# The 31-tap depthwise convolution of a three-block network: which engines compute its four channel pairs

## The chip, the cores and the metric

One core of one Trainium2 chip runs the whole program. The metric is the time of one execution on the device in microseconds (us), the median of several. A core has five engines with queues of their own: TensorE (PE: matrix multiplication, with weight loads shown as PEld), VectorE (DVE), ScalarE (ACT), GpSimd (POOL) and SyncE (SP, which here only issues DMAs). They run side by side and order each other by semaphores.

## The reference, cut to what matters

The network is three blocks on 256 positions and 1024 channels, all float32. The change lies in the first block's second layer, a Conformer convolution module:

```python
def conformer_conv(h, pw1_w, pw1_b, dw_w, dw_b, ln_g, ln_b, pw2_w, pw2_b):
    u = h @ pw1_w + pw1_b
    a, gt = jnp.split(u, 2, axis=-1)
    c = causal_dwconv(a * jax.nn.sigmoid(gt), dw_w, dw_b)
    c = jax.nn.silu(layernorm(c, ln_g, ln_b))
    return c @ pw2_w + pw2_b
```

`causal_dwconv` has 31 taps for each channel: output position t is the sum over s of 0 to 30 of the input at t-s times the tap weight of that channel for s. The layer norm goes over the channels, so it needs the convolution of all 1024 channels before it can start.

## The kernel before, in words

Activations lie feature-major in SBUF: a tile is 128 channels by 256 positions, and the 1024 channels are eight tiles, in four pairs q = 0 to 3 (tiles 2q and 2q+1). Nearly all buffers are 256-wide slices of one SBUF tensor, the arena. Weights of 1 MB units stream from HBM through a ring of eight slots (`weight_ring`). SP issues a unit as soon as PE has used up the unit whose slot it takes. The third block ends in a mixture of 64 experts whose weights stream through the same ring and through the arena in transfers of 2 MB.

The order on each engine is written out by hand. In the Conformer stage it is this.

PE (`conf_pe`, L1431): the gated projection pw1 in eight column pairs (the first two in a sweep while the norm before it ends, L1432, then pairs 2 to 7, L1433 to L1435). Even pairs are the gate, odd pairs the value; value pair 2q+1 completes channel pair q. Then a projection of the memory that a later attention needs (`xa_k1` pair 2, L1436). Then the convolution of channel tiles 6 and 7 as matrix products (L1439 to L1442): for each tap and tile a diagonal matrix of the tap's weights, times the shifted input, summed in PSUM bank 4. Then two more memory projections (`xa_k1` 3, `xa_v1` 0), the products with a matrix of ones that sum all eight convolved tiles for the mean (L1446 to L1452), `xa_v1` 1, the sums of squares (L1454, `norm_pe` L398), and pw2.

ACT: for each q a sigmoid of the gate (L1477), and for q = 0 to 2 the base of the convolution, `conf_base_act` (L1457): input times the weight of the tap s=0, plus the bias, into the tile pair `CV`. The 62 diagonal matrices (two tiles by 31 taps) are built by ACT much earlier, in the feed-forward stage (L1344, `diag`). After the products ACT takes the two tiles out of PSUM (L1485).

DVE (`conf_dve`, L1534): for each q the gated product (`glu_dve`, L1509) and behind it a portion of the convolution of pairs 0 to 2 (`conv_taps_dve`, L1514). Each of the 30 further taps is two scalar_tensor_tensor instructions, one for each tile of the pair: tile += shifted input times tap weight, both inputs in SBUF (L1526). Before each tap DVE waits for its own tap before (`own.wait()`). In total 180 such instructions. Then come the mean (L1542), its subtraction (L1546) and the layer norm.

POOL (`conf_pool`, L1157): only the short sums of squares of the norms (`sums_pool`, L315); between the two norms of the stage it has nothing.

The semaphores `cv_base` (base of pair q is there), `conv_mm`, `conv_out`, `cv_ready` (a pair is complete on DVE) and `mean_mm` order these steps. `CB0` (L1284) is the count of `conv_base` at which the second feed-forward starts, 35 while the diagonals count for one.

Of the kernel before, what the change touches and what calls it, by code (L numbers as in the profile page):

```python
# [17 lines left out]
ACT = mybir.ActivationFunctionType  # L18
ALU = mybir.AluOpType
AX = mybir.AxisListType  # L20

P = 128
# [161 lines left out]
def program(nc, io):  # L184
    with ExitStack() as ctx:
# [32 lines left out]
        def vec(name, i, n=1):  # L218
            return VT[:, VEC[name] + i:VEC[name] + i + n]
# [936 lines left out]

        def conf_pool(pool, own):  # L1157
            sums_pool(pool, own, "b1_1_in")
            sums_pool(pool, own, "b1_1_mix")


# [119 lines left out]


        FF, UG, UV = 0, 22, 26
        CB0 = {0: 12, 1: 35}  # L1284

        def branch(base, q):
            return lambda j: A[:, base + 2 * (q % 2) + j, :]
# [27 lines left out]
        def ffn_act(act, own, l):  # L1315
            name = f"ffn_in{l}"
            squares_act(act, f"ff_in{l}", x_after(f"xa_out{l}"))
            std_act(act, f"ff_in{l}")
            for p in range(23):
                if p < 22:  # L1320
                    q = p // 2
                    if p < 2:
                        wait_evac(act, name, p)
                    else:
                        wait_pair(act, name, p)
                    src = conv_source(name, p)
                    if q >= 2:
                        act.wait_ge(sem["ff_ready"], 11 * l + q - 1)
                    col = (22 if p % 2 else 0) + 2 * q
                    for j in range(2):  # L1330
                        ins = nc.scalar.activation(branch(UV if p % 2 else UG, q)(j), src[:, j, :], ACT.Identity,  # L1331
                                                   bias=vec("ffn_cb", 44 * l + col + j),
                                                   scale=vec("ffn_cw", (3 * l + 2) * 44 + col + j))
                    ins.then_inc(sem["conv_base"], 1)
                if p % 2 == 1:
                    q = p // 2
                    wait_conv(act, l, p - 1)
                    u = A[:, UG + 2 * (q % 2):UG + 2 * (q % 2) + 2, :]
                    nc.scalar.activation(u, u, ACT.Silu).then_inc(sem["sg_ready"], 1)
            if l == 0:  # L1340
                act.wait_ge(sem["ff_ready"], 11)
                for t in range(2):
                    for k in range(CF_K):
                        ins = nc.scalar.activation(diag(t, k), ident, ACT.Identity, scale=vec("dw_w", k * 8 + 6 + t))  # L1344
                ins.then_inc(sem["conv_base"], 1)
            else:
                tables_act(act, 0)
                act.wait_ge(sem["lam_mm"], 1)
                nc.scalar.activation(LAME, PB[6][:, 0:8], ACT.Exp).then_inc(sem["lam_exp"], 1)
            post_act(act, f"ff_out{l}", f"ffn_out{l}")  # L1350
            std_act(act, f"ff_out{l}")
            if l == 0:
                memory_copy_act(act, *FILL["ff_out0"])
# [54 lines left out]
        CIN, CV, SIG, SWEPT1 = 0, 8, 16, 84  # L1408
        cvt = tiles(CV)
        MEAN = A[:, 20, :]  # L1410
        CONV_Q = 3
        CONV_PART = 13

        def diag(t, k):

            at = (22 if t == 0 else 38) + k // 2
            if at >= 48:
                at += 8
            return A[:, at, k % 2 * P:k % 2 * P + P]

        def pw1_swept(p):
            return A[:, SWEPT1 + 2 * p:SWEPT1 + 2 * p + 2, :]
# [8 lines left out]
        def conf_pe(pe):  # L1431
            sweep_pe(pe, "b1_1_in", [("pw1", 0), ("pw1", 1)], 4)  # L1432
            for p in range(2, 8):  # L1433
                for m in range(2):
                    half_pe(pe, "pw1", p, m, ht, ready=h_after("b1_1_in") if p == 2 else None)  # L1435
            memory_pe(pe, "xa_k1", 2)  # L1436
            wait_glu(pe, 3)
            pe.wait_ge(sem["conv_base"], CB0[1])
            for j in range(2):  # L1439
                for s in range(CF_K):  # L1440
                    mm = nc.tensor.matmul(PB[4][:, j * T + s:j * T + T], diag(j, CF_K - 1 - s), A[:, CIN + 6 + j, 0:T - s],  # L1441
                                          start=(s == 0), stop=(s == CF_K - 1))  # L1442
            mm.then_inc(sem["conv_mm"], 1)
            memory_pe(pe, "xa_k1", 3)
            memory_pe(pe, "xa_v1", 0)
            for n, t in enumerate((6, 7, 0, 1, 2, 3, 4, 5)):  # L1446
                if t >= 6:
                    pe.wait_ge(sem["conv_out"], 1)
                else:
                    pe.wait_ge(sem["cv_ready"], t // 2 + 1)  # L1450
                mm = nc.tensor.matmul(PB[6][:, 0:T], ones, cvt(t), start=(n == 0), stop=(n == 7))
            mm.then_inc(sem["mean_mm"], 1)  # L1452
            memory_pe(pe, "xa_v1", 1)
            norm_pe(pe, "ln")  # L1454
            out_pe(pe, "b1_1_mix", "pw2", cvt, lambda e, kc: e.wait_ge(sem["ln_out"], kc + 1))
# [8 lines left out]
        def conf_act(act, own):  # L1464
            squares_act(act, "b1_1_in", x_after("ff_out0"))
            std_act(act, "b1_1_in")
            for q in range(4):
# [9 lines left out]
                    ins = nc.scalar.activation(A[:, SIG + 2 * (q % 2) + j, :], src[:, j, :], ACT.Sigmoid,  # L1477
                                               bias=vec("pw1_b", 8 + 2 * q + j))
                ins.then_inc(evac[b] if q else sem["swept_gate"], 1)
                if q < CONV_Q:  # L1480
                    conf_base_act(act, q)
            memory_copy_act(act, "xa_k1", 2)
            act.wait_ge(sem["conv_mm"], 1)
            for j in range(2):
                ins = nc.scalar.activation(cvt(6 + j), PB[4][:, j * T:j * T + T], ACT.Identity, bias=vec("dw_b", 6 + j))  # L1485
            ins.then_inc(sem["conv_out"], 1)
            memory_copy_act(act, "xa_k1", 3)
            memory_copy_act(act, "xa_v1", 0)
            norm_act(act, "ln", cvt, lambda e, t: e.wait_ge(sem["centered"], t // 4 + 1))
            memory_copy_act(act, "xa_v1", 1)  # L1490
            for t in range(8):
# [19 lines left out]
                                                     in1=A[:, SIG + 2 * (q % 2) + j, :], op0=ALU.add, op1=ALU.mult)  # L1511
            ins.then_inc(evac[b] if q else sem["swept_conv"], 1)

        def conv_taps_dve(dve, own, lo, hi):  # L1514

            taps = CF_K - 1
            for n in range(lo, hi):
                q, s = n // taps, n % taps + 1
                if s == 1:
                    wait_glu(dve, q)  # L1520
                    dve.wait_ge(sem["cv_base"], q + 1)
                else:
                    own.wait()
                for j in range(2):
                    t = 2 * q + j
                    ins = nc.vector.scalar_tensor_tensor(  # L1526
                        out=cvt(t)[:, s:T], in0=A[:, CIN + t, 0:T - s], scalar=vec("dw_w", (CF_K - 1 - s) * 8 + t),
                        in1=cvt(t)[:, s:T], op0=ALU.mult, op1=ALU.add)
                    if s < taps:
                        own(ins)  # L1530
                if s == taps:
                    ins.then_inc(sem["cv_ready"], 1)

        def conf_dve(dve, own):  # L1534
# [2 lines left out]
                scaled_dve(dve, "pw1", p, pw1_swept(p))  # L1537
            for q in range(4):
                glu_dve(dve, q)
                conv_taps_dve(dve, own, CONV_PART * q, CONV_PART * q + CONV_PART if q < 3 else CONV_Q * (CF_K - 1))  # L1540
            dve.wait_ge(sem["mean_mm"], 1)
            own(nc.vector.tensor_scalar(MEAN, PB[6][:, 0:T], 1.0 / D, None, ALU.mult))  # L1542
            own.wait()
# [1821 lines left out]
```

## Time and profile before

| | us |
|---|---|
| median of 3 runs | 3311.75 (3311.26 to 3314.72) |
| the profiled execution | 3312.16 |
| its span in the trace | 3310.4 |
| PE busy | 3240.6 (98%) |
| DVE busy | 865.4 (26%) |
| ACT busy | 660.8 (20%) |
| POOL busy | 245.5 (7%) |
| mean granted TensorE clock | 0.995 of full speed |

The page of the profile gives busy times for the whole span. The Conformer stage is only a short part of it (about 645 to 805 us of the span), so the stage is read by the chain of waits, the timelines of single engines, and the tables of one source line. In a timeline a row is a start, a length, the engine and line, the operation with its tiles, how many instructions were merged into it, and in brackets how long the engine had sat idle before and what ended that.

### The profile page before, as it was taken

To read this page: it belongs to the slowest core of one execution; us is meant where nothing else is said; L and a number is where in the kernel's file an instruction comes from. 1 tells how busy PE (TensorE), PEld (TensorE's weight loads), DVE (VectorE), ACT (ScalarE), POOL (GpSimd) and SP (SyncE) were. 2 spreads that over 40 slices of the span, in tenths; PEclk is the share of its full clock that TensorE was granted. 3 is DMA by queue.
4 is the path that set the end of the run, shared out by engine and by line. 5 is a ranking of instruction groups with operands and counts; after the bars stand their busy time and mean duration, and the time that the engine had idled before them with its cause. 6 is when DMAs were issued, how large, how long until landed. Compare 5 with 4: busy or idle time off the path is not lost.

```text
span 3310.4 us, 38838 instructions
## 1 busy us (share of the span) xinstructions
PE 3240.6 (98%) x15862; PEld 2450.7 (74%) x15862; DVE 865.4 (26%) x1873; ACT 660.8 (20%) x1172; POOL 245.5 (7%) x203
## 2 busy tenths in 40 slices
PE   8999999999999999999999999999999999999998
PEld 7888888888888878888778888788655444554444
DVE  4532232294332243002330024432211111111111
ACT  3531123112221043001220023340111111111111
POOL 0110010000000110100111011210000000000000
PEclk9999999999999999999999999999999999999999
DMA  5233344433243432444324434225699999999996
GB/s 221 101 131 136 127 149 144 153 115 121 97 165 131 149 126 108 160 143 153 112 109 165 141 139 173 82 94 191 249 429 429 428 429 428 429 429 428 428 429 269
DMA packets 71222, 714.93 MB, mean 216 GB/s; under 512 B 7968, under 2 KB 7968, under 8 KB 9152
## 3 DMA queue, kind: packets, MB, share of 16 engines
q1 hardware_dynamic: 70416, 710.06, 54.2%
q0 software_dynamic: 688, 3.15, 0.3%
q8 instruction: 92, 1.51, 0.2%
q14 instruction: 26, 0.21, 0.0%
HBM read 712.13 MB, written 1.05 MB: 215 GB/s over the span
## 4 chain that ended last, share of the span: by engine, by line
PE 87%; DMA 8%; DVE 3%; ACT 1%; issue 1%; POOL 0%; SPq 0%; DVEq 0%; ACTq 0%
PE bank L265 50%; PE bank L3002 10%; PE bank L284 8%; DMA weight_ring<-in_experts 8%; PE bank L3033 5%; PE bank L2987 3%; PE bank L2979 2%; PE bank L2227 1%; PE bank L1441 1%; DVE residual L1099 1%; PE bank L467 0%; PE bank L1205 0%; PE bank L1185 0%; PE bank L738 0%; PE bank L324 0%
## 5 line engine op out<-in xcount | busy, mean ns | idle before, releaser
L265 PE MATMUL bank<-normed_residual,weight_ring 128*128 128x256 f32 x4192 | 920.8, 380 | 0.0
L265 PEld LDWEIGHTS bank<-normed_residual,weight_ring 128*128 128x128 f32 x4192 | 792.3, 190 | 115.4 <-issue 10.4
L265 PE MATMUL bank<-arena,weight_ring 128*128 128x256 f32 x2920 | 641.1, 382 | 4.7 <-ACT arena L1493 3.9
L265 PEld LDWEIGHTS bank<-arena,weight_ring 128*128 128x128 f32 x2920 | 558.4, 192 | 82.7 <-issue 4.8
L3002 PE MATMUL bank<-weight_ring,arena 128*64 128x512 f32 x1024 | 227.5, 593 | 2.8 <-DMA weight_ring<-in_experts 2.8
L284 PE MATMUL bank<-gained_residual,weight_ring 128*128 128x256 f32 x896 | 205.2, 389 | 23.7 <-DVE gained_residual L358 12.0
L3002 PE MATMUL bank<-arena 128*64 128x512 f32 x1024 | 225.2, 592 | 2.3 <-DVE arena L3080 2.3
L3033 PE MATMUL bank<-weight_ring,arena 128*64 128x512 f32 x992 | 219.7, 595 | 0.0
L284 PEld LDWEIGHTS bank<-gained_residual,weight_ring 128*128 128x128 f32 x896 | 174.5, 196 | 51.0 <-DVE gained_residual L358 14.0
L3002 PEld LDWEIGHTS bank<-weight_ring,arena 128*64 128x64 f32 x1024 | 72.7, 137 | 152.3 <-issue 139.5
L3002 PEld LDWEIGHTS bank<-arena 128*64 128x64 f32 x1024 | 73.6, 137 | 148.0 <-issue 148.0
L3086 DVE TENSOR_TENSOR arena<-bank,arena 128x512 f32<-128x512 f32 x32 | 22.1, 692 | 613.9 <-PE bank L3002 613.9
L384 ACT ACTIVATE arena<-bank 128x512 f32<-128x512 f32 x121 | 72.1, 596 | 462.9 <-PE bank L265 462.8
L3033 PEld LDWEIGHTS bank<-weight_ring,arena 128*64 128x64 f32 x992 | 68.5, 137 | 127.6 <-issue 123.9
L315 POOL TENSOR_TENSOR arena<-arena 128x512 f32<-128x512 f32 x51 | 71.6, 1403 | 1144.8 <-ACT arena L344 597.4
L2987 PEld LDWEIGHTS bank<-arena 128*128 128x128 f32 x528 | 97.6, 190 | 39.5 <-issue 26.0
L2987 PE MATMUL bank<-arena 128*128 128x256 f32 x528 | 122.8, 386 | 0.7 <-ACT arena L3059 0.7
L1369 DVE SCALAR_TENSOR_TENSOR arena<-bank,vectors,arena 128x255 f32<-128x255 f32 (+1 forms) x160 | 69.8, 478 | 202.5 <-ACT arena L1331 201.1
L2979 PE MATMUL bank<-arena 128*128 128x128 f32 x1024 | 119.7, 275 | 1.0 <-DVE arena L3066 1.0
L2979 PEld LDWEIGHTS bank<-arena 128*128 128x128 f32 x1024 | 116.9, 192 | 1.8 <-DVE arena L3066 1.8
L284 PE MATMUL bank<-arena,weight_ring 128*128 128x256 f32 x512 | 115.4, 381 | 1.2 <-ACT arena L488 1.2
L284 PEld LDWEIGHTS bank<-arena,weight_ring 128*128 128x128 f32 x512 | 96.0, 190 | 16.5 <-issue 2.4
(387 smaller groups left out, 2543.6 us busy)
## 6 DMA issues: line engine op xcount, KB each, us to landing
weight_ring<-in_stream SPq DMA_DIRECT2D x290, 1024.0 KB, 4.8
weight_ring<-in_experts SPq DMA_DIRECT2D x126, 2048.0 KB, 18.6
arena<-in_experts SPq DMA_DIRECT2D x66, 2048.0 KB, 18.4
residual<-in_x SPq DMA_DIRECT2D x1, 1024.0 KB, 4.7
arena<-in_mem POOLq DMA_DIRECT2D x1, 1024.0 KB, 5.1
out<-gained_residual SPq DMA_DIRECT2D x4, 256.0 KB, 2.4
constants<-in_con SPq DMA_DIRECT2D x1, 612.5 KB, 7.1
vectors<-in_vec SPq DMA_DIRECT2D x1, 548.5 KB, 6.0
```

Source lines behind the costliest of these rows:

```text
L265: mm = nc.tensor.matmul(PB[b][:, m * T:m * T + T], l, r, start=(kc == 0), stop=(kc == chunks - 1))
L284: mm = nc.tensor.matmul(PB[b][:, m * T:m * T + T], W[:, u % SLOTS, kc, m * P:m * P + P], src(kc), start=(kc == first and m == 0), stop=(kc ...
L315: ins = nc.gpsimd.tensor_tensor(A[:, base:base + 2, :], A[:, base:base + 2, :], A[:, base + 2 * p:base + 2 * p + 2, :], ALU.add)
L384: nc.scalar.activation(dst, bank(b), func).then_inc(evac[b], 1)
L1099: nc.vector.tensor_tensor(x, x, m, ALU.add).then_inc(sem["x_final"], 1)
L1369: ins = nc.vector.scalar_tensor_tensor(out=d[:, s:T], in0=src[:, j, 0:T - s], scalar=vec("ffn_cw", (3 * l + 2 - s) * 44 + col + j), in1=d[ ...
L1441: mm = nc.tensor.matmul(PB[4][:, j * T + s:j * T + T], diag(j, CF_K - 1 - s), A[:, CIN + 6 + j, 0:T - s], start=(s == 0), stop=(s == CF_K ...
L2227: mm = nc.tensor.matmul(PB[2 + n // 4][:, n % 4 * P:n % 4 * P + P], l, r, start=True, stop=True)
L2979: mm = nc.tensor.matmul(PB[k // 4][:, k % 4 * PAIR:(k % 4 + 1) * PAIR], HTOK[:, c, k * P:k * P + P], GSEL[:, c, :], start=(c == 0), stop=( ...
L2987: mm = nc.tensor.matmul(PB[4 + d // 2][:, d % 2 * T:d % 2 * T + T], YEX[:, d * P:d * P + P], SPREAD, start=False, stop=True, skip_group_ch ...
L3002: mm = nc.tensor.matmul(PB[w][rows, :], GATHERED[:, 4 * half + k, rows], tile[:, k, :], start=(half == 0 and k == 0), stop=(half == 1 and ...
L3033: mm = nc.tensor.matmul(PB[3 - j][rows, :], HIDT[:, k, rows], tile[:, k, :], start=(k == 0), stop=(k == 3))
```

## The change

Pairs 0 and 2 (tiles 0, 1, 4, 5) are now computed by ACT and POOL together: for each of the 30 further taps ACT multiplies the two tiles by the tap's weights (two instructions) into one of four product buffers, and POOL adds the pair of products to the pair of tiles in one tensor_tensor add of 128 partitions by 2 x (256-s) elements. Each add waits for the add before it and for its product; each product waits until its buffer has been added. Pairs 1 and 3 stay on DVE, in the form they had. The 62 diagonal matrices, the 124 matrix products and ACT's two copies out of PSUM are gone. PE's sums for the mean now take the tiles in the order 0 to 7, so each pair in turn is waited for.

```diff
         def conf_pool(pool, own):
             sums_pool(pool, own, "b1_1_in")
+            conv_adds_pool(pool)
             sums_pool(pool, own, "b1_1_mix")
...
-        CB0 = {0: 12, 1: 35}
+        CB0 = {0: 12, 1: 34}
...
-            if l == 0:
-                act.wait_ge(sem["ff_ready"], 11)
-                for t in range(2):
-                    for k in range(CF_K):
-                        ins = nc.scalar.activation(diag(t, k), ident, ACT.Identity, scale=vec("dw_w", k * 8 + 6 + t))
-                ins.then_inc(sem["conv_base"], 1)
-            else:
+            if l == 1:
...
-            wait_glu(pe, 3)
-            pe.wait_ge(sem["conv_base"], CB0[1])
-            for j in range(2):
-                for s in range(CF_K):
-                    mm = nc.tensor.matmul(PB[4][:, j * T + s:j * T + T], diag(j, CF_K - 1 - s), A[:, CIN + 6 + j, 0:T - s],
-                                          start=(s == 0), stop=(s == CF_K - 1))
-            mm.then_inc(sem["conv_mm"], 1)
...
-            for n, t in enumerate((6, 7, 0, 1, 2, 3, 4, 5)):
-                if t >= 6:
-                    pe.wait_ge(sem["conv_out"], 1)
+            for t in range(8):
+                if t // 2 in POOL_PAIRS:
+                    pe.wait_ge(sem["conv_out"], TAPS * (POOL_PAIRS.index(t // 2) + 1))
                 else:
-                    pe.wait_ge(sem["cv_ready"], t // 2 + 1)
-                mm = nc.tensor.matmul(PB[6][:, 0:T], ones, cvt(t), start=(n == 0), stop=(n == 7))
+                    pe.wait_ge(sem["cv_ready"], DVE_PAIRS.index(t // 2) + 1)
+                mm = nc.tensor.matmul(PB[6][:, 0:T], ones, cvt(t), start=(t == 0), stop=(t == 7))
...
-                if q < CONV_Q:
+                if q < 3:
                     conf_base_act(act, q)
+                if q:
+                    conv_products_act(act, 10 * q - 10, 10 * q)
+            conf_base_act(act, 3)
+            conv_products_act(act, 30, 40)
             memory_copy_act(act, "xa_k1", 2)
-            act.wait_ge(sem["conv_mm"], 1)
-            for j in range(2):
-                ins = nc.scalar.activation(cvt(6 + j), PB[4][:, j * T:j * T + T], ACT.Identity, bias=vec("dw_b", 6 + j))
-            ins.then_inc(sem["conv_out"], 1)
+            conv_products_act(act, 40, 46)
             memory_copy_act(act, "xa_k1", 3)
+            conv_products_act(act, 46, 52)
             memory_copy_act(act, "xa_v1", 0)
+            conv_products_act(act, 52, 60)
...
+        def conv_products_act(act, lo, hi):
+            for n in range(lo, hi):
+                q, s = POOL_PAIRS[n // TAPS], n % TAPS + 1
+                if n == TAPS:
+                    wait_glu(act, q)
+                if n >= PRODS:
+                    act.wait_ge(sem["conv_out"], n - PRODS + 1)
+                for j in range(2):
+                    t = 2 * q + j
+                    ins = nc.scalar.activation(prod(n)[:, j, s:T], A[:, CIN + t, 0:T - s], ACT.Identity,
+                                               scale=vec("dw_w", (TAPS - s) * 8 + t))
+                ins.then_inc(sem["conv_mm"], 1)
+
+        def conv_adds_pool(pool):
+            for n in range(2 * TAPS):
+                q, s = POOL_PAIRS[n // TAPS], n % TAPS + 1
+                if s == 1:
+                    pool.wait_ge(sem["cv_base"], q + 1)
+                if n:
+                    pool.wait_ge(sem["conv_out"], n)
+                pool.wait_ge(sem["conv_mm"], n + 1)
+                c = A[:, CV + 2 * q:CV + 2 * q + 2, s:T]
+                nc.gpsimd.tensor_tensor(c, c, prod(n)[:, :, s:T], ALU.add).then_inc(sem["conv_out"], 1)
...
             for q in range(4):
                 glu_dve(dve, q)
-                conv_taps_dve(dve, own, CONV_PART * q, CONV_PART * q + CONV_PART if q < 3 else CONV_Q * (CF_K - 1))
+                if 1 <= q < 3:
+                    conv_taps_dve(dve, own, 0, 13 * q - 12, 13 * q + 1)
+            conv_taps_dve(dve, own, 0, 27, TAPS + 1)
+            conv_taps_dve(dve, own, 1, 1, TAPS + 1)
```

## Rows read from the trace of the kernel before

**Rows 1.** The page, part 1: busy us (share) xinstructions of each engine.
```profile
PE 3240.6 (98%) x15862; PEld 2450.7 (74%) x15862; DVE 865.4 (26%) x1873; ACT 660.8 (20%) x1172; POOL 245.5 (7%) x203
```
**Rows 2.** Chain of waits, Conformer stage: start us, length us, what.
```profile
663.16 48.35 PE bank L265 x224
711.51 25.21 PE bank L1441 x124
736.72 13.81 PE bank L265 x64
750.53 3.45 PE bank L1451 x16
753.99 6.91 PE bank L265 x32
760.89 3.47 PE bank L398 x16
```
**Rows 3.** Chain of waits, expert stage, first and last of ten DMA pieces.
```profile
2988.86 25.43 DMA weight_ring<-in_experts
...
3252.99 25.58 DMA weight_ring<-in_experts
```
**Rows 4.** Waits of SP's DMA queue, 2250 to 2420 us: total, times, longest.
```profile
SPq L3135 <- PE bank L265: 42.4, 3, 16.0
```
**Rows 5.** Timeline of DVE, Conformer stage.
```profile
678.76 11.34 DVE L1526 SCALAR_TENSOR_TENSOR arena<-arena,vectors 128x242 f32<-128x242 f32 x26
690.89 0.88 DVE L1509 SCALAR_TENSOR_TENSOR arena<-bank,vectors,arena 128x256 f32<-128x256 f32 x2 [0.79 <-PE bank L265]
...
705.50 44.78 DVE L1526 SCALAR_TENSOR_TENSOR arena<-arena,vectors 128x246 f32<-128x246 f32 x102
```
**Rows 6.** ACT: the diagonals by line (ns min/median/max, first and last start), one base pair.
```profile
L1344 ACT ACTIVATE arena<-constants,vectors x62: 385/386/401, 566.4 to 584.2; 128x128 f32<-128x128 f32 x62
...
678.88 1.09 ACT L1460 ACTIVATE arena<-arena,vectors 128x256 f32<-128x256 f32 x2 [7.94 <-DVE arena L1509]
```
**Rows 7.** POOL's groups by form: busy us, mean ns, then idle before.
```profile
L2072 POOL TENSOR_TENSOR arena<-arena 128x512 f32<-128x512 f32 x32 | 33.3, 1045 | 184.0 <-ACT arena L384 151.6 <-DVE arena L2058 32.4
...
L605 POOL TENSOR_TENSOR arena<-arena 128x512 f32<-128x512 f32 x2 | 2.5, 1267 | 0.2
...
L605 POOL TENSOR_TENSOR arena<-arena 128x256 f32<-128x256 f32 x1 | 0.7, 728 | 0.1
```
**Rows 8.** Timelines of POOL and DVE, 197 to 202 us: a chain of adds.
```profile
198.53 1.54 POOL L1007 TENSOR_TENSOR arena<-arena 128x512 f32<-128x512 f32 x1
...
200.21 1.27 POOL L1007 TENSOR_TENSOR arena<-arena 128x512 f32<-128x512 f32 x1
...
201.63 1.26 POOL L1007 TENSOR_TENSOR arena<-arena 128x512 f32<-128x512 f32 x1
...
197.82 1.12 DVE L942 TENSOR_TENSOR arena<-arena 128x512 f32<-128x512 f32 x1 [1.97 <-ACT arena L384]
```
**Rows 9.** Timelines of POOL and DVE, 652 to 655 us.
```profile
652.61 1.63 POOL L315 TENSOR_TENSOR arena<-arena 128x512 f32<-128x512 f32 x1 [1.29 <-ACT arena L344]
...
652.43 0.68 DVE L1097 TENSOR_TENSOR arena<-arena,rstd 128x512 f32<-128x512 f32 x1
653.15 1.64 DVE L1099 TENSOR_TENSOR residual<-residual,arena 128x512 f32<-128x512 f32 x1
```
**Rows 10.** Lines L1402 (POOL) and L1099 (DVE): ns min/median/max, starts, forms.
```profile
L1402 POOL TENSOR_TENSOR arena<-arena x22: 1262/1265/1323, 428.9 to 1053.4; 128x512 f32<-128x512 f32 x22
...
L1099 DVE TENSOR_TENSOR residual<-residual,arena x24: 691/1163/1643, 272.4 to 1145.5; 128x512 f32<-128x512 f32 x24
```
**Rows 11.** PE after an idle time: timeline row, and stretch with busy times, clock.
```profile
282.98 2.07 PE L324 MATMUL bank<-arena,constants 128*128 128x256 f32 x4 [4.22 <-POOL arena L315]
284.85 7.51 PE L265 MATMUL bank<-arena,weight_ring 128*128 128x256 f32 x27
...
282.00:286.00 4.00, 3.02 (x7) 2.46 (x8) 0.40 (x1) 0.55 (x2) 0.93 (x1) 0.50 0.25 107
```

More of the change, by code:

```diff
@@ L1410, in program @@
         MEAN = A[:, 20, :]
[L1411 to L1419, printed above, removed]
+        POOL_PAIRS, DVE_PAIRS = (0, 2), (1, 3)
+        TAPS, PRODS, CPROD = CF_K - 1, 4, 22
         def pw1_swept(p):
@@ L1512, in glu_dve, with prod, conv_taps_dve @@
             ins.then_inc(evac[b] if q else sem["swept_conv"], 1)
-        def conv_taps_dve(dve, own, lo, hi):
-            taps = CF_K - 1
+        def prod(n):
+            return A[:, CPROD + 2 * (n % PRODS):CPROD + 2 * (n % PRODS) + 2, :]
+        def conv_products_act(act, lo, hi):
             for n in range(lo, hi):
-                q, s = n // taps, n % taps + 1
+                q, s = POOL_PAIRS[n // TAPS], n % TAPS + 1
[18 more added lines that the diff above has]
+                nc.gpsimd.tensor_tensor(c, c, prod(n)[:, :, s:T], ALU.add).then_inc(sem["conv_out"], 1)
+        def conv_taps_dve(dve, own, n, lo, hi):
+            q = DVE_PAIRS[n]
+            for s in range(lo, hi):
                 if s == 1:
@@ L1523, in conv_taps_dve @@
                     own.wait()
-                for j in range(2):
-                    t = 2 * q + j
+                for t in (2 * q, 2 * q + 1):
                     ins = nc.vector.scalar_tensor_tensor(
-                        out=cvt(t)[:, s:T], in0=A[:, CIN + t, 0:T - s], scalar=vec("dw_w", (CF_K - 1 - s) * 8 + t),
+                        out=cvt(t)[:, s:T], in0=A[:, CIN + t, 0:T - s], scalar=vec("dw_w", (TAPS - s) * 8 + t),
                         in1=cvt(t)[:, s:T], op0=ALU.mult, op1=ALU.add)
-                    if s < taps:
+                    if s < TAPS:
                         own(ins)
-                if s == taps:
+                if s == TAPS:
                     ins.then_inc(sem["cv_ready"], 1)
```

## The prediction

> **What bounds the kernel now.** The page comes first: TensorE is busy for 98% of the span and every other engine for at most 26% [rows 1]. That says that removing matrix products may pay, not where. So the next view is the chain of waits in the Conformer stage. It runs over PE without a gap: projections from 663.16, the 124 diagonal products for 25.21 us from 711.51, two memory projections (13.81 us), the sums for the mean (3.45 us) from 750.53 to 753.99 [rows 2]. Then comes the timeline of DVE: the 180 tap instructions are packed too, and the last run of 102 begins at 705.50 and lasts 44.78 us, to 750.28 [rows 5]. The reader is to see that the mean starts at 750.5 for two reasons at once: PE is through with its projections at 750.53, and DVE has its last tap 0.25 us earlier. Taking 25 us from PE gains nothing unless the convolution is ready earlier as well. From 754 on, PE, DVE and ACT follow one another on the chain, so the finish of the mean sets everything behind it.
>
> Does a shift there reach the end of the kernel? In the last 300 us the chain is one of expert weight transfers, 25.4 us each, ten of them [rows 3]. These could hide a delay if they started by themselves. But SP issues the first of them only as PE's dense products (L265) free the slots: it waited 42.4 us for that line [rows 4]. So a delay in the Conformer stage moves the start of the stream by the same amount, and I count it one to one.
>
> **What is removed.** 25.21 us of matrix products [rows 2]. PE would be through with pw1 and the three memory projections at 750.53 - 25.21 = 725.3. The 62 diagonals on ACT (566.4 to 584.2, rows 6) lie beside the down projection of the feed-forward, in which PE is never short of work; I cost their removal at nothing, and the order of ACT's later work there is unchanged. ACT's wait for PSUM goes too, and is off the path.
>
> **What is added on ACT.** 120 products. A diagonal of 128 columns, with the same kind of scale, starts every 17.8/61 = 0.29 us; a base pair of 256 columns, with scale and bias, takes 1.09 us for two [rows 6]. So a tap costs between 0.6 and 1.1 us; I take 0.9, nearer the base, which has the same width. Sixty taps are 54 us, in a window of over 100. ACT can't set the pace as long as the add is dearer. What queues behind a product that waits for its buffer: the sigmoid of pair 3, whose bank `xa_v1` 0 wants at 725.3 - 6.9 = 718.4 (ACT is there about four adds ahead of POOL, near 711), and the copies of the three memory projections, whose banks PE wants only behind the mean. I cost both at nothing; a late sigmoid would be hidden by the wait for the adds.
>
> **What is added on POOL.** 60 adds in one chain. A tensor_tensor takes 1267 ns at 128x512 and 728 ns at 128x256, 2.1 ns an element [rows 7]. The mean tap has 2 x 240.5 = 481 elements: 1267 - 31 x 2.1 = 1.20 us. Between an add and the next that waits for it lie 201.63 - (200.21 + 1.27) = 0.15 us [rows 8]. The period is 1.35 us, and 60 periods are 81 us. That alone is more than the whole time there was: the products can't begin before the gated product of pair 1, since ACT's in-order queue has them behind that base. PE finishes value pair 3 at 663.16 + 64 x 0.216 = 677.0 (48.35/224 = 0.216 each, rows 2); DVE's gated product takes 0.88 [rows 5], the base 1.09 [rows 6], the first product 0.9. POOL starts at 680.0. The cheapest row for such a width is 1045 ns, an instruction that reads one tile twice [rows 7]; that is the lower bound, 0.98 + 0.15 = 1.13 us a period.
>
> **What is left on DVE.** 120 tap instructions at 0.44 us each (11.34/26, 44.78/102; rows 5) instead of 180: 53 us, from 679.1 on. Undisturbed it would be done near 735.
>
> **What they do to each other.** This is the dearest term, and the totals of busy time don't show it. Both DVE's tap and POOL's add read two tiles in SBUF. At 652.61 POOL began an add while a DVE instruction with two SBUF inputs was under way to 653.11: the add took 1.63 instead of 1.27 us. DVE's next started at 653.15 and took 1.64 instead of 0.69: it ended 0.55 after the add had ended at 654.24 [rows 9]. It had made no progress meanwhile. The spread of these two lines is the same story: L1402, with no such neighbour, stays at 1.26 to 1.32 us, L1099 lies between 0.69 and 1.64 [rows 10]. In a chain of adds, a DVE instruction caught at 197.82 took 1.12 us and ended 0.55 behind the add that ended at 198.39, and the next add took 1.54 instead of 1.27 [rows 8]. So they take turns, and a DVE instruction of 512 elements costs the next add 0.27 us. One of 240 elements reads for half as long (0.25 of 0.53 us, estimated from the 0.55), and that fits into what lies between two adds: the 0.15, and the first 0.1 of the add (1.54 - 1.27 = 0.27 of delay where DVE ended 0.41 after the add had started). The second tap instruction starts 0.4 us after the first and finds the add running. So while POOL adds, DVE gets about one instruction for each add, and POOL keeps about its 1.35 us.
>
> The Trainium skill, "SBUF — State Buffer", section "Who interferes with whom", says this in general: a VectorE instruction with two SBUF inputs contends with a GpSimd instruction that reads SBUF, as an exclusive lock held for the whole instruction. The rows above agree (0.69 became 1.64 us). Without the lock the sum would be 3324, with it held as strictly as the rule reads, 3376; both are worked out from rows under the rivals.
>
> **The sum.** POOL does ten adds from 680.0 to 693.5; DVE, with a start of two instructions, has 12 of its 26 up to the next gated product, and needs 14 x 0.44 = 6.2 us more: 699.7. The gated product of pair 2 (0.88), the base (1.09) and a product bring POOL's next start to 702.5. Twenty adds end at 729.5, with 24 of DVE's 26; then 0.9 for two taps, and 0.88 + 1.09 + 0.9 before POOL goes on at 733.2, as ACT has the products from 30 on behind the base of pair 3. Thirty adds: 773.7. DVE then has 34 of its last 68 to do: 15.0 us, to 788.7. The sums over tiles 6 and 7 are a quarter of 3.45 [rows 2]: the mean is ready at 789.6, against 753.99. That is +35.6.
>
> PE has by then been idle, but for a few sums, since 725.3. After an idle time of 4.22 us its granted clock was 0.50, and 27 products took 7.51 instead of 5.83 us, the four before them 2.07 instead of 1.13 [rows 11]: together 2.6 us, and at 6.8 us of half clock 3.4 is the most those rows allow. `xa_v1` 1 and the sums of squares stand behind the mean on PE, on the path [rows 2], so this counts in full: +3.4. Its bounds are 0 and 3.4 by these rows; a much longer idle time has no row here. Together +39: 3311.75 + 39 = 3351. The profiled execution lay 0.4 above the median, so its changed form would be near 3351 too (span near 3349.5).
>
> If DVE gets both instructions of a tap behind each add, the period becomes 1.35 + 0.26 to 1.35 + 0.4 us, POOL is never starved after the first stop, and both end between 782 and 790 together. So the sum hardly depends on who wins each turn; it is 3344 to 3352.
>
> **The rivals.**
> - *Strict turns.* Each add waits for two whole tap instructions and nothing fits in between: 1.35 + 2 x 0.44 = 2.23 us a tap, 134 us for sixty, to 813.8. The mean at 814.7 is +60.7, with the clock +64: 3376. For it: the 1.63 and 1.64 us of rows 9. Against it: in rows 8 the add lost 0.27, not 0.69.
> - *No contention.* If tap instructions with a pointer scalar passed beside adds, as no row here shows, DVE would be done at 735 and POOL at 680 + 81 = 761. The last four tiles' sums take 1.7: mean at 762.8, +8.8, with the clock +12: 3324. Against it speak rows 8 to 10, for tensor_tensor on DVE; scalar_tensor_tensor also reads two SBUF tiles.
> - *Not slower.* If there is no contention and the adds run at the rate of the cheapest POOL row, 1.13 us a period, POOL waits at 691.3 for the base of pair 2 (693.5) and is done at 750.0; mean at 751.8, 2.2 before 753.99, and with a clock loss of 1.7 to 3.4 this is 3311 to 3313. The point from which it decides is the period: below about 1.13 us the change doesn't lose. Against it: the instructions with two different tiles in rows 7, 8 and 10 stand at 1.26 or more.
>
> **How the numbers follow.** The forecast has 0.68; strict turns 0.16; no contention 0.13; not slower 0.03. The likeliest case has 3338 to 3362, with the bounds of the clock, of the products and of who wins. The range goes up to take in strict turns, 3338 to 3378, and leaves out the last two cases, 0.16. A measurement of this kernel can tell about 0.2% (6.6 us) from no change. Slower by more than that has 0.96, within it 0.03, faster 0.01.
>
> **What would show it.** In the timeline of the changed kernel: PE with no work of length from about 725 to about 789. POOL's add line with 60 instructions, a mean of 1.2 to 1.3 us by this forecast (2 us or more in strict turns), and two stops of 3 to 9 us. DVE's tap instructions at over 1 us each beside adds and 0.47 alone. The last DVE tap after the last add. A half clock behind the mean. The prediction is wrong if taps stay at 0.47 us beside adds, or if POOL starts well before 680.

## The result, and the profile after

| | before | after |
|---|---|---|
| median, us | 3311.56 (3311.26 to 3314.72, 4 runs) | 3349.77 (3348.42 to 3350.4, 4 runs) |
| span of the profiled execution, us | 3310.4 | 3347.5 |
| granted TensorE clock | 0.995 | 0.985 |

The ratio is 1.0113, with a 95% interval of 1.0095 to 1.013: the change costs 38 us. The prediction was 3351, range 3338 to 3378.

The line of busy times of the changed kernel's page, against [rows 1]. PE has 20 us less to do, DVE 30 us more although it has 60 instructions less, and that is the first sign that DVE's instructions got longer.

```profile
PE 3221.1 (96%) x15738; PEld 2429.0 (73%) x15738; DVE 895.1 (27%) x1813; ACT 693.2 (21%) x1230; POOL 320.6 (10%) x263
```

The chain of waits of the changed kernel from the end of pw1's pair 3 to the sums of squares, against [rows 2] (start us, length us, what). L1537 is the tap on DVE, L1432 the sums for the mean.

```profile
676.16 0.89 DVE arena L1493 x2
677.07 1.10 ACT arena L1441 x2
678.26 0.89 DVE arena L1537 x2
679.18 2.88 DVE arena L1537 x2
...
769.54 2.50 DVE arena L1537 x2
772.07 0.86 DVE arena L1537 x2
...
785.14 0.83 DVE arena L1537 x2
786.01 2.07 PE bank L1432 x4
788.08 7.51 PE bank L265 x32
795.59 3.47 PE bank L398 x16
```

Before, this stretch was PE's from end to end. Now it is DVE's for 108 us. A row of it is the two instructions of one tap, one for each tile of the pair; below, counts and times "a tap" on DVE are of one such instruction. Two of them take 2.5 to 2.9 us as long as POOL adds, and 0.83 to 0.86 from 772 on, when POOL is through. The mean is ready at 788.08 instead of 753.99.

POOL's and DVE's timelines of the same stretch, against [rows 5] for DVE (L1525 is the add, L1493 the gated product).

```profile
679.10 13.72 POOL L1525 TENSOR_TENSOR arena<-arena 128x510 f32<-128x510 f32 x10 [23.23 <-ACT arena L1511]
702.21 25.98 POOL L1525 TENSOR_TENSOR arena<-arena 128x490 f32<-128x490 f32 x20 [9.39 <-ACT arena L1511]
731.70 40.08 POOL L1525 TENSOR_TENSOR arena<-arena 128x510 f32<-128x510 f32 x30 [3.50 <-ACT arena L1511]
...
678.26 21.11 DVE L1537 SCALAR_TENSOR_TENSOR arena<-arena,vectors 128x255 f32<-128x255 f32 x26 [1.23 <-ACT arena L1441]
...
700.07 28.75 DVE L1537 SCALAR_TENSOR_TENSOR arena<-arena,vectors 128x242 f32<-128x242 f32 x26
...
729.53 56.42 DVE L1537 SCALAR_TENSOR_TENSOR arena<-arena,vectors 128x229 f32<-128x229 f32 x68
```

POOL works in three runs of 10, 20 and 30 adds with two stops of 9.39 and 3.50 us between them, each of which ends when ACT, which had waited for DVE's gated product, delivers a product. Two source lines over 735 to 769 us and over the taps behind the last add show the price of one instruction (ns min/median/max):

```profile
L1537 DVE SCALAR_TENSOR_TENSOR arena<-arena,vectors x26: 1246/1354/1479, 734.7 to 768.2; 128x255 f32<-128x255 f32 x2, 128x254 f32<-128x254 f32 x2, 128x253 f32<-128x253 f32 x2, 128x252 f32<-128x252 f32 x2
...
L1537 DVE SCALAR_TENSOR_TENSOR arena<-arena,vectors x30: 445/458/469, 773.0 to 785.5; 128x240 f32<-128x240 f32 x2, 128x239 f32<-128x239 f32 x2, 128x238 f32<-128x238 f32 x2, 128x237 f32<-128x237 f32 x2
```

26 tap instructions in 34 us, 1.3 us for each: as many as there are adds. That answers to the single meetings of [rows 8, 9].

At the end of the kernel the expert transfers are on the chain as in [rows 3], the last at 3290.03 instead of 3252.99: the shift arrives whole.

```profile
3290.03 25.58 DMA weight_ring<-in_experts
```

### The profile page after: what moved, and what is told of

The parts are those of the page before. It is cut to its first block, busy times and chain, and to the rows that moved or that the text cites. A ratio compares the mean times of both kernels' runs of the same rounds, so it can differ in the third digit from the quotient of the medians.

```text
span 3347.5 us, 38707 instructions
## 1 busy us (share of the span) xinstructions
PE 3221.1 (96%) x15738; PEld 2429.0 (73%) x15738; DVE 895.1 (27%) x1813; ACT 693.2 (21%) x1230; POOL 320.6 (10%) x263
## 4 chain that ended last, share of the span: by engine, by line
PE 83%; DMA 9%; DVE 7%; ACT 1%; issue 1%; POOL 0%; SPq 0%; DVEq 0%; ACTq 0%
PE bank L265 48%; PE bank L3016 10%; DMA weight_ring<-in_experts 8%; PE bank L284 8%; PE bank L3047 4%; DVE arena L1537 3%; PE bank L3001 2%; PE bank L2993 2%; PE bank L2241 1%; DVE residual L1099 1%; PE bank L467 0%; PE bank L1206 0%; PE bank L1186 0%; PE bank L738 0%; PE bank L324 0%
```

## The experiments

**Which part takes the time: adds cut to one column.**

```diff
-                c = A[:, CV + 2 * q:CV + 2 * q + 2, s:T]
-                nc.gpsimd.tensor_tensor(c, c, prod(n)[:, :, s:T], ALU.add)
+                c = A[:, CV + 2 * q:CV + 2 * q + 2, s:s + 1]
+                nc.gpsimd.tensor_tensor(c, c, prod(n)[:, :, s:s + 1], ALU.add)
```

> The changed kernel with POOL's 60 adds cut to one column of each tile (the sums of pairs 0 and 2 are left out but for that column); ACT's products and DVE's 120 tap instructions stay. Theory (POOL's adds and DVE's taps take turns at SBUF): the taps fall to 0.44 us each throughout, no 1.4 us ones are left; DVE is then bound by the gated products of pairs 2 and 3 and ends near 734 us of the span, mean near 736, time near 3295 (before: 3311.6). Rival (ACT's products, which read and write SBUF all the time, slow the taps): taps stay near 1.4 us beside products and the time stays near 3350.

Measured: 3299.75 us, ratio to before 0.9962 (0.9947 to 0.9978). ACT's products were all there. DVE's timeline of this kernel:

```profile
677.96 11.69 DVE L1537 SCALAR_TENSOR_TENSOR arena<-arena,vectors 128x255 f32<-128x255 f32 x26 [1.23 <-ACT arena L1441]
...
708.75 26.53 DVE L1537 SCALAR_TENSOR_TENSOR arena<-arena,vectors 128x255 f32<-128x255 f32 x60 [1.08 <-ACT arena L1441]
```

26 taps in 11.69 us and 60 in 26.53: 0.44 to 0.45 us each. The products don't slow DVE; the adds do. The mean came at 737.3, about 1 us later than expected, and the time is 4.7 us above the expectation; where the rest of that lies wasn't looked into.

**The adds without taps beside them: taps cut to one column.**

```diff
-                        out=cvt(t)[:, s:T], in0=A[:, CIN + t, 0:T - s], ...
-                        in1=cvt(t)[:, s:T], ...
+                        out=cvt(t)[:, s:s + 1], in0=A[:, CIN + t, 0:1], ...
+                        in1=cvt(t)[:, s:s + 1], ...
```

> The changed kernel with DVE's 120 tap instructions cut to one column each (the convolution of pairs 1 and 3 is left out but for that column); POOL's adds stay whole. Theory: the adds keep a period of 1.35 us, so POOL alone needs 60 x 1.35 = 81 us from 679 and ends near 760; mean near 763, time near 3322: the kernel is still slower than before without any contention. Rival (the adds were slow only because of the taps): a period near 1.13 us, end near 750, time near 3311.

Measured: 3327.66 us, ratio 1.0045 (1.0029 to 1.0061). POOL's last run of this kernel:

```profile
697.24 63.62 POOL L1525 TENSOR_TENSOR arena<-arena 128x490 f32<-128x490 f32 x50 [3.36 <-ACT arena L1511]
```

63.62/50 = 1.27 us a period, of which the add itself has a median of 1.21. So the chain of 60 adds alone makes the kernel slower than before. The expected period of 1.35 was too long: between two chained adds lie 0.08 us here, not 0.15. The time is 5.7 us above the expectation all the same. Some of that shows: a first stop of 3.36 us that I had put at nothing (two tiny taps took 1.1 us beside an add, so the gated product of pair 2 was late, at 694.33), eight sums at half clock (3.78 us), and a whole stage that lay 1.6 us later than in the changed kernel from its beginning on.

One-column taps aren't free of the adds either, but for each add two of them pass and not one (the instructions around 691.27 us):

```profile
690.04 1.24 POOL L1525 TENSOR_TENSOR arena<-arena 128x496 f32<-128x496 f32 x1
690.14 1.28 DVE L1537 SCALAR_TENSOR_TENSOR arena<-arena,vectors 128x1 f32<-128x1 f32 x2
...
691.35 1.23 POOL L1525 TENSOR_TENSOR arena<-arena 128x494 f32<-128x494 f32 x1
```

The first of the two waits out the add (690.14 to 691.29), the second takes 0.21 us, as they do with POOL at rest, and has begun 0.14 us before the next add does.

**Taking the meeting away: DVE's accumulators in PSUM.**

```diff
+        def cacc(t):
+            q = t // 2
+            return PB[4 + DVE_PAIRS.index(q)][:, t % 2 * T:t % 2 * T + T] if q in DVE_PAIRS else cvt(t)
...
-                        out=cvt(t)[:, s:T], in0=A[:, CIN + t, 0:T - s], ...
-                        in1=cvt(t)[:, s:T], ...
+                        out=cacc(t)[:, s:T], in0=A[:, CIN + t, 0:T - s], ...
+                        in1=cacc(t)[:, s:T], ...
...
+                    own.wait()
+                    nc.vector.tensor_copy(A[:, CV + 2 * q:CV + 2 * q + 2, :], bank(4 + n)).then_inc(sem["cv_ready"], 1)
```

> The changed kernel with DVE's accumulators of pairs 1 and 3 in two free PSUM banks instead of SBUF: ACT writes the base there, each tap reads one SBUF tile and one PSUM tile, a copy of 128x512 brings each pair back. Nothing is left out. Theory: with one SBUF input the taps no longer take turns with the adds: 0.44 to 0.48 us each, DVE ends near 737, POOL is the last and ends near 760; time near 3322, the price of one_column_taps. Rival (any two instructions of DVE and POOL that touch SBUF hinder each other, writes included): taps stay over 1 us beside adds, time 3340 or more.

Measured: 3321.88 us, ratio 1.0029 (1.0017 to 1.0041). POOL and DVE of this kernel:

```profile
694.32 63.69 POOL L1529 TENSOR_TENSOR arena<-arena 128x490 f32<-128x490 f32 x50 [0.59 <-ACT arena L1515]
...
716.55 26.48 DVE L1541 SCALAR_TENSOR_TENSOR bank<-arena,vectors,bank 128x255 f32<-128x255 f32 x60 [6.45 <-ACT bank L1445]
743.06 0.69 DVE L1547 COPY arena<-bank 128x512 f32<-128x512 f32 x1
```

Both run at full speed beside each other, 0.44 us a tap and 1.27 a period, with the whole work done. What they fought for is the accumulator's access to SBUF: its read as the tap's second SBUF input, or its write, for this kernel moves both to PSUM. That it is the read is shown by the last kernel of this section. There the last tap of pair 1 reads one tile in SBUF and one in PSUM and writes to SBUF, beside an add of POOL (709.02 to 710.25), and takes no longer than the same form at 736.06 with POOL at rest:

```profile
709.13 0.87 DVE L1542 SCALAR_TENSOR_TENSOR arena<-arena,vectors,bank 128x255 f32<-128x255 f32 x2
```

This is the cause made and unmade: the contention is worth 3349.77 - 3321.88 = 28 us of the 38, and what is left, 10 us, is POOL's chain.

The Trainium skill, "SBUF — State Buffer", section "Who interferes with whom", has the rule for both sides: two SBUF inputs contend with a GpSimd instruction that reads SBUF, while at most one, outside certain fast modes of VectorE, doesn't. The runs agree (1.35 against 0.44 us a tap). The same page, section "Summary: rules for kernel authors", says that the second to issue is blocked until the first finishes. For DVE that holds here: the tap waits out the add. The add behind a tap lost only 0.05 us on average (76.9 us for the 60 adds here, 79.8 in the changed kernel). Single instructions show why (an add of the changed kernel with the tap that was under way at its start, and the same with taps of twice the length, from the kernel with double taps below):

```profile
736.12 1.47 DVE L1537 SCALAR_TENSOR_TENSOR arena<-arena,vectors 128x255 f32<-128x255 f32 x1
737.39 1.30 POOL L1525 TENSOR_TENSOR arena<-arena 128x502 f32<-128x502 f32 x1
...
730.01 1.63 DVE L1538 SCALAR_TENSOR_TENSOR arena<-arena,vectors 128x504 f32<-128x504 f32 x1
731.17 1.58 POOL L1525 TENSOR_TENSOR arena<-arena 128x508 f32<-128x508 f32 x1
```

In the first pair the tap runs 0.20 us into the add, and the add takes 0.05 longer than the same add of the PSUM kernel (1.25); in the second it is 0.46 us, and 0.32 longer than 1.26. Over all adds that met a tap the loss is the overlap less 0.14 us: 0.19 and 0.05 on average in the changed kernel, 0.43 and 0.29 with the long taps, 0.41 and 0.27 in [rows 8]. So the add does wait for the tap, but only until 0.14 us before the tap's recorded end.

**Was PE ever what the stage waited for? The kernel before, without its products.**

```diff
-                for s in range(CF_K):
-                    mm = nc.tensor.matmul(PB[4][:, j * T + s:j * T + T], diag(j, CF_K - 1 - s), A[:, CIN + 6 + j, 0:T - s],
-                                          start=(s == 0), stop=(s == CF_K - 1))
+                mm = nc.tensor.matmul(PB[4][:, j * T:j * T + T], diag(j, CF_K - 1), A[:, CIN + 6 + j, 0:T],
+                                      start=True, stop=True)
```

> The kernel before with its 124 diagonal products cut to one tap for each of the two tiles (the other 30 taps of tiles 6 and 7 are left out). My reading of before: DVE's last tap at 750.28 binds next, so the mean comes 1.9 to 2.8 us earlier, less what a low clock after PE's idle time of about 24 us costs: time 3309 to 3312. Rival (the products were what the stage waited for, the reason to take them off PE): up to 24 us less, 3288.

Measured: 3312.9 us, ratio 1.0001 (0.999 to 1.0011). PE of this kernel, with the sums for the mean in two parts:

```profile
726.68 2.75 PE L1450 MATMUL bank<-arena,constants 128*128 128x256 f32 x12
750.96 2.08 PE L1450 MATMUL bank<-arena,constants 128*128 128x256 f32 x4 [21.52 <-DVE arena L1525]
752.83 8.84 PE L265 MATMUL bank<-weight_ring,arena 128*128 128x256 f32 x32
```

24 us of matrix products gone, and nothing gained: PE now waits 21.52 us for DVE's tap, and pays the low clock behind the wait (8.84 us for the projection, 7.07 in the same timeline row of the kernel before). The mean comes 1.6 us earlier against the beginning of the stage, and the clock takes that back; the time is 0.9 us above the expected range. The products of [rows 2] had been work in DVE's shadow.

**The clock term: PE kept busy in its waits.** Matrix products of constants into an unread bank, 8, 10, 78 and 26 of them ahead of the four waits for pairs.

```diff
+                if t % 2 == 0:
+                    for _ in range((8, 10, 78, 26)[t // 2]):
+                        nc.tensor.matmul(PB[5][:, 0:T], ones, CT[:, 0:T], start=True, stop=True)
```

> The changed kernel with idle matrix products (122 of 256 columns, constants, into a bank that nobody reads) in PE's waits for the convolution, so that PE isn't idle before the mean. It sizes the clock term, 3.4 us in the prediction and 1.5 by the traces of the two kernels. Theory: the last four sums take 1.1 us instead of 2.07, the memory projection behind them 6.9 to 7.1 instead of 7.7; mean about 1 us earlier, time near 3348. Rival (the full 3.4 us was there, spread over more of the stage): time near 3346.

Measured: 3346.55 us in one run. The last sums took 1.13 us (2.07 in the changed kernel) and the projection 7.07 (7.72):

```profile
786.22 1.13 PE L1435 MATMUL bank<-arena,constants 128*128 128x256 f32 x4
787.19 7.07 PE L265 MATMUL bank<-weight_ring,arena 128*128 128x256 f32 x32
```

From the last sum of the norm ahead of the stage to that of the norm behind it the changed kernel needs 851.25 - 655.93 = 195.3 us, this one 849.98 - 655.96 = 194.0. The clock costs 1.3 us in the stage. One run doesn't decide between the two expected times (it is nearer the rival's), but the stage does: not 3.4. The rest of the 2.8 us by which the spans differ comes on far behind. The stretches of 11 us from the first expert products on (the changed kernel, this one, the kernel before; length, busy us and count of PE, PEld, DVE, ACT, POOL, clock, DMA) are:

```profile
2403.00:2414.00 11.00, 10.68 (x42) 3.57 (x44) 1.08 (x5) 0.00 (x0) 0.00 (x0) 0.84 0.38 128
...
2402.00:2413.00 11.00, 10.68 (x50) 3.79 (x52) 1.07 (x5) 0.10 (x1) 0.00 (x0) 1.00 0.53 198
...
2368.00:2379.00 11.00, 10.52 (x50) 3.79 (x52) 1.23 (x5) 0.00 (x0) 0.00 (x0) 1.00 0.51 191
```

The granted clock is 0.84 in the changed kernel and 1.00 in the two others, which is worth about 0.16 x 11 = 1.8 us (15.65 - 13.96 = 1.7 in the first group of products). The PSUM kernel shows the same there: its first 32 products take 8.78 us, 7.09 before. Why the clock is low at this place in some of the kernels isn't shown.

**What sets the end: POOL's start moved forward.** One edit on ACT's order: products 0 to 4 behind the base of pair 0, 4 to 8 ahead of that of pair 1.

```diff
+                if q == 1:
+                    conv_products_act(act, 4, 8)
                 if q < 3:
                     conf_base_act(act, q)
-                if q:
-                    conv_products_act(act, 10 * q - 10, 10 * q)
+                if q == 0:
+                    conv_products_act(act, 0, 4)
...
```

> The changed kernel with one edit on ACT's order: the products of pair 0 start right behind its base, at 665 instead of 678 us, while DVE has no tap to do. Both accumulators stay in SBUF. Theory (turns: each of POOL's adds lets one tap through, and the end is the sum of both engines' work): some 10 adds are done before DVE's first tap, 10 taps run at 0.44 instead of 1.38 us, DVE ends near 776 instead of 785.5; time near 3340. Rival (DVE's chain alone sets the end, POOL's start doesn't matter): 3350.

Measured: 3342.67 us, ratio 1.0093 (1.0076 to 1.011). POOL began at 667.5 instead of 679.1 and did eight adds alone; DVE's mean step came at 781.84 instead of 788.12, in an execution whose stage began 1.2 us later. So 7.1 us less in the time for 11.6 us of an earlier start. The end isn't DVE's chain alone; it depends on how many adds meet taps. The time is 2.7 us above the expected 3340: POOL had stops of 2.25, 11.19 and 5.24 us for the bases in ACT's order, more than with the old order.

**What passes between two adds: taps of half the width, taps of twice the length.**

```diff
-                        out=cvt(t)[:, s:T], in0=A[:, CIN + t, 0:T - s], ...
-                        in1=cvt(t)[:, s:T], ...
+                w = (T - s) // 2
...
+                        out=cvt(t)[:, s:s + w], in0=A[:, CIN + t, 0:w], ...
+                        in1=cvt(t)[:, s:s + w], ...
```

> The changed kernel with each of DVE's 120 tap instructions on half of its columns (the other half of pairs 1 and 3 gets the base alone). It asks what passes between two adds: one instruction, or so much of the interface's time. Theory (one instruction for each add, since the second starts too late): beside adds still one tap instruction per add, near 1.35 us each; only those that run alone get shorter (0.34 instead of 0.44), so the mean comes about 6 us earlier, time near 3344. Rival (a share by elements): two half taps per add, DVE ends with or before POOL near 762, time near 3326.

```diff
-                for t in (2 * q, 2 * q + 1):
+                for t in (2 * q,):
+                    c = A[:, CV + t:CV + t + 2, s:T]
                     ins = nc.vector.scalar_tensor_tensor(
-                        out=cvt(t)[:, s:T], in0=A[:, CIN + t, 0:T - s], ...
+                        out=c, in0=A[:, CIN + t:CIN + t + 2, 0:T - s], ...
```

> The changed kernel with one DVE instruction for both tiles of a tap (the odd tile of pairs 1 and 3 gets the even tile's weights, so its own weights are left out); the same number of elements in 60 instructions of twice the length. Theory (one instruction for each add, whatever its length): a whole tap passes behind each add, each add waits about 0.3 us longer, period 1.6 us; POOL's adds and DVE's last tap end together near 781, mean about 5 us earlier than in the changed kernel, time near 3344. Rival (the interface's time is shared by elements, so the cut into instructions doesn't matter): adds and taps as in the changed kernel, time near 3350.

Measured: 3338.75 us (ratio 1.0076, 1.0047 to 1.0105) for the half taps, 3342.55 us (1.0088, 1.0058 to 1.0117) for the double ones. Beside these two the kernel before took 3313.72 us, 2 more than beside the others, so the ratios are the better comparison: the changed kernel has 1.0113 (1.0095 to 1.013), from which the double taps aren't clear by time. What decides is the traces. The chain of waits of the first, and POOL's long run of the second:

```profile
681.48 2.66 DVE arena L1538 x2
684.14 0.02 issue
684.17 2.63 DVE arena L1538 x2
```

```profile
699.67 76.38 POOL L1525 TENSOR_TENSOR arena<-arena 128x490 f32<-128x490 f32 x50 [4.12 <-ACT arena L1511]
```

A tap of half the columns still takes 1.3 us beside adds, one instruction for each add. And 60 instructions of twice the length bring both tiles of a tap through behind each add, at an add period of 76.38/50 = 1.53 us. So from 127 to 510 columns what is shared out is turns, not elements. That isn't a count kept for each add, as the one-column taps show, of which two pass: the second half tap begins about 0.01 us before the next add (740.56 and 740.57) and has to wait it out, the second one-column tap 0.14 us before it and passes. The half taps gained about twice what I expected (11 to 12 us, not 6). Against the changed kernel POOL's runs got shorter too: 13.21, 25.21 and 38.38 us against 13.72, 25.98 and 40.08, together 3 us. So a full tap does delay an add, by 0.05 us on average; that of a half one is not seen. And the taps that ran alone followed each other every 0.31 us instead of the expected 0.34.

**A version from these parts.** DVE's accumulators in PSUM (but the last tap of a pair writes to SBUF), POOL's chain from the base of pair 0 on, ten taps of pair 0 on DVE in the 11 us in which it had nothing to do, and PE's sums for the mean in the order in which the pairs become ready. The diff shows the additions on DVE and the split; the order of ACT's products changes too.

```diff
+        def at_pool(n):
+            return (0, n + 1) if n < TAKEN else (2, n - TAKEN + 1)
...
+        def part_dve(dve, own):
+            wait_glu(dve, 0)
+            for s in range(TAKEN + 1, TAPS + 1):
...
+        def merge_dve(dve):
+            dve.wait_ge(sem["conv_out"], TAKEN)
+            c = A[:, CV:CV + 2, TAKEN + 1:T]
+            nc.vector.tensor_tensor(c, c, bank(6)[:, :, TAKEN + 1:T], ALU.add).then_inc(sem["cv_ready"], 1)
```

> All of the convolution is computed. DVE accumulates in PSUM (no turns with POOL, as psum_accumulators showed) with the last tap of a pair written to SBUF; the products start right behind the base of pair 0 (about 12 us earlier); of pair 0 POOL adds taps 1 to 20 and DVE takes taps 21 to 30 in the time in which it has nothing else, in a third PSUM bank, and merges them by one add; pairs 1 and 3 on DVE, pair 2 on POOL. Theory: POOL's 50 adds at 1.27 us are over near 730, DVE near 735, mean near 737 instead of 754; time near 3298, faster than both kernels. Rival (ACT, whose queue now has bases, sigmoids and products in one order, starves POOL or DVE): POOL ends behind 745 and the time is 3305 or more.

Measured: 3299.84 us, ratio 0.9964 (0.995 to 0.9978): 11.5 us faster than before and 50 faster than the changed kernel, with the whole convolution computed.

```profile
681.50 53.99 POOL L1529 TENSOR_TENSOR arena<-arena 128x494 f32<-128x494 f32 x42 [2.84 <-ACT arena L1515]
...
736.06 0.87 DVE L1542 SCALAR_TENSOR_TENSOR arena<-arena,vectors,bank 128x255 f32<-128x255 f32 x2
```

POOL's last add ends at 735.49, DVE's last tap at 736.93, PE was through at 726: three engines within 11 us. POOL was held up for 2.84 us once, as ACT's next products stand behind the base of pair 1, and that had to wait for its gated product. There is a little left in that, and in giving PE a few taps again; neither was tried.

## Why the prediction was right

*The bound before.* Right. The step "taking 25 us from PE gains nothing unless the convolution is ready earlier as well" is the fourth experiment: 3312.9 us.

*POOL's start and its stops.* Right within 1 us, with the whole stage 0.9 us earlier than in the profile of before (655.93 against 656.85 for the last sums of the norm ahead of it, before any changed work of the stage; the same four sums at 283 us took 2.07 us at low clock before [rows 11] and 1.13 after, which is as much). Forecast less 0.9: starts at 679.1, 701.6 and 732.3; measured 679.10, 702.21 and 731.70.

*The period of the adds.* The sum had 1.35 us; measured 1.37, 1.30 and 1.34. That is in part luck, for two errors nearly cancelled: the time between chained adds is 0.08 and not the 0.15 of [rows 8], and taps delay an add by about 0.05, which I had at nothing. Why the chain of [rows 8] had twice the gap stays open; it waits for two semaphores as this one does.

*What passes beside an add.* Right, and it was the decisive term. "About one instruction for each add" is seen in the changed kernel, in half taps and in double ones. The step from 512 elements in a tensor_tensor [rows 8, 9] to 240 in a tap with a pointer scalar held. The reason given was right in kind and off in its parts: a tap runs 0.27 us past the add that it waited out (0.25 in the estimate), of which 0.08 and not 0.15 lie between the adds, and 0.14 and not 0.1 more cost the next add nothing.

*The DVE rest.* Forecast 15.0 us for 34 instructions behind the last add; measured 32 of them, from 772.07 to 785.97, 13.9. With the start shifted, the last tap came 1.8 us earlier than the sum had it.

*The clock.* The term that was mis-sized in the stage: 3.4 us taken, 1.3 measured by filling the waits. I had taken the most that the rows allow; the 6.8 us of half clock in that sentence come from the granted clocks 0.89, 0.50 and 0.76 of three stretches of 4 us from 278 on, of which [rows 11] show the second alone. PE's earlier short sums lie inside the wait and off the path; for the last four and the projection 2.07 + 7.51 us were used for what costs 1.13 + 6.91 at full clock. Another 1.7 us of low clock came in the expert stage, where the prediction had none, so that its total for the clock is nearly met for a reason that it didn't give.

*One to one to the end.* Right in the main. The shift is 34.6 us behind the stage (816.62 to 851.25), 34.1 at the norm near 1310, 34.8 at the first expert product (2368.48 to 2403.32), and 37.1 at the end. What came on in the expert stage begins with the first group of products, 15.65 us instead of 13.96, which is the low clock named above; the remaining 0.6 wasn't looked into. Against its own beginning, 0.9 earlier, the stage cost 35.5 us where the sum had 39.0: DVE's last tap came 1.8 us sooner, and the clock took about 2 less. (The mean came 35.0 us later where the sum had 35.6, but the 35.0 include 0.9 of low clock in the last sums.) Some 2.3 us came on far behind the change. That the total of 38 is within 1 us of the forecast 39 is therefore in part luck: the stage alone was overrated by 3.5.

*The rivals.* "No contention" was priced at 3324 and is the PSUM kernel: 3321.9. "Strict turns" fell because one instruction passes for each add and not two. "Not slower" needed a period of 1.13 us; alone the adds have 1.27. The side case of both instructions of a tap behind each add, put at 3344 to 3352, is what the double taps make: a period of 1.53 us and 3342.6.

## What to carry to other kernels

Before work is moved from a busy engine to idle ones, look which engine ends just behind it: here 25 us of matrix products lay in the shadow of DVE's taps, and their removal alone was worth nothing. When POOL and DVE are to work side by side, look at the operands and not at the busy shares: a DVE instruction of 127 to 510 columns with two SBUF inputs got one turn for each POOL add here, so two thirds of its speed can go (0.44 to 1.35 us), while one of the two inputs in PSUM left both at full speed, for the price of a copy of 0.69 us for each pair. A long chain on POOL must begin with its first input, and work should be cut so that the engines end together.

## What the runs showed of the hardware that I had not expected

Beside adds of 1.2 us a tap of 255 columns takes 1.35 us and one of 127 columns 1.3 us, while one of 2 x 255 columns takes a median of 1.53 us: one for each add. Of DVE instructions of a single column, with two SBUF inputs, two pass for each add, one in 1.1 to 1.2 us and one in 0.21. An add that finds a tap under way waits until 0.14 us before the tap's recorded end, with taps of about 240 columns as with those of about 480.

The granted clock of the changed kernel in the long wait (start and end, length, busy us and count of PE, PEld, DVE, ACT, POOL, clock, DMA):

```profile
732.00:785.00 53.00, 4.15 (x8) 2.35 (x8) 51.97 (x61) 25.92 (x60) 37.50 (x30) 0.50 0.00 0
```

Fifty us with hardly any work on PE, at the lower of its two levels (0.50, 1.2 GHz), but the price behind it was no higher than behind the 4 us of [rows 11]: 1.3 us in the stage against 2.6. Behind the 21.52 us of the kernel before without its products it was 0.9 for the sums and 1.8 for the projection, 2.7 in all. So the price doesn't grow with the length of the wait in these three cases; what sets it isn't shown.
